# Probabilities times values in one fp32 product: the attention stages of a two-layer encoder trunk without the split of P

## The reference

```
layer 0: u = rms_norm(h)
         z = u @ ab_w_in                  -> q and kv latents, gates, q/k/v of branch B
  "mla": 8 heads, q and k of 96, v of 64, key chunk <= query chunk (64-token chunks)
  "chk": 8 heads, q, k and v of 64, each chunk sees itself and 8 chunks before, plus a bias
         h += [o_a * silu(g_a), o_b * silu(g_b)] @ ab_w_out
layer 1: q, k, v, g, f = rms_norm(h) @ fox_w_in
  "fox": 16 heads of 64, causal, scores + cum[q] - cum[k]
         h += (o_c * silu(g_c)) @ fox_w_out
both:    o = softmax(scores) @ v
         h += (p @ pe_w) * sigmoid(rms_norm(h) @ pe_gate_w)
```

## Time and profile before

| what | value |
|---|---|
| median of three runs | 1998.39 us |
| the profiled execution, and its span | 1996.7 us, 1994.9 us |
| mean granted TensorE clock | 0.956 |
| PE busy | 1783.1 us (89%), 12720 matmuls |
| PE weight loads busy | 1637.5 us (82%) |
| VectorE, ScalarE, GpSimd busy | 955.8 us (48%), 827.3 us (41%), 98.3 us (5%) |
| attention stages, first score to the next stage's first matmul | mla 455 to 625, chk 625 to 800, fox 1460 to 1764 |

### The profile page before, as it was taken

How to read it: one execution, slowest core, us unless ns; L and a number is a source line. 1 busy time by engine, 2 the same in 40 slices (tenths; PEclk the granted TensorE clock), 3 DMA queues, 4 the chain that set the end, 5 groups by cost and what they waited for, 6 DMA issues and landing times. The chain is left out here.

```text
span 1994.9 us, 31875 instructions
## 1 busy us (share of the span) xinstructions
PE 1783.1 (89%) x12720; PEld 1637.5 (82%) x12720; DVE 955.8 (48%) x1797; ACT 827.3 (41%) x1702; POOL 98.3 (5%) x55
## 2 busy tenths in 40 slices
PE   5999778988996996999989999999968988869998
PEld 5999767867884775999988999998757777769898
DVE  5454556105774665234345444331057777722631
ACT  4433234215773675123153332312157878711410
POOL 0000000000210111000000000000002112100000
PEclk9999989998996998999999999999989999989999
DMA  5054468416424551510123433453174555251111
GB/s 179 22 197 143 119 160 220 122 56 171 127 75 111 138 129 42 184 54 27 49 106 106 127 123 119 131 138 102 45 178 122 142 138 129 64 180 48 64 64 38
DMA packets 178372, 223.94 MB, mean 112 GB/s; under 512 B 12857, under 2 KB 148297, under 8 KB 178225
## 3 DMA queue, kind: packets, MB, share of 16 engines
q1 hardware_dynamic: 177152, 218.43, 38.1%
q0 software_dynamic: 640, 2.62, 0.4%
q10 hardware_dynamic: 432, 0.85, 0.1%
HBM read 150.34 MB, written 77.29 MB: 114 GB/s over the span
## 5 line engine op out<-in xcount | busy, mean ns | idle before, releaser
L1562 PE MATMUL m_acc<-m_w_hi,g_a_hi 128*128 128x256 f32 (+1 forms) x1280 | 370.6, 290 | 19.0 <-DVE m_w_lo L179 14.6
L1562 PE MATMUL m_acc<-m_w_hi,g_a_lo 128*128 128x256 f32 (+1 forms) x1280 | 365.5, 286 | 0.0
L1562 PE MATMUL m_acc<-m_w_lo,g_a_hi 128*128 128x256 f32 (+1 forms) x1280 | 364.6, 285 | 0.0
L1562 PEld LDWEIGHTS m_acc<-m_w_hi,g_a_hi 128*128 128x128 f32 x1280 | 246.0, 192 | 19.4 <-DVE m_w_lo L179 14.7
L1562 PEld LDWEIGHTS m_acc<-m_w_lo,g_a_hi 128*128 128x128 f32 x1280 | 246.8, 193 | 0.0
L1562 PEld LDWEIGHTS m_acc<-m_w_hi,g_a_lo 128*128 128x128 f32 x1280 | 244.6, 191 | 0.0
L611 PE MATMUL pa_acc<-pa_w_hi,g_a_hi 128*128 128x256 f32 (+2 forms) x512 | 156.4, 305 | 15.9 <-DVE pa_w_lo L179 15.9
L1562 PE MATMUL t_acc<-t_w_hi,g_a_hi 128*128 128x256 f32 x512 | 146.9, 287 | 15.2 <-DVE t_w_lo L179 15.2
L611 PE MATMUL pa_acc<-pa_w_hi,g_a_lo 128*128 128x256 f32 (+2 forms) x512 | 151.8, 297 | 0.0
L611 PE MATMUL pa_acc<-pa_w_lo,g_a_hi 128*128 128x256 f32 (+2 forms) x512 | 151.5, 296 | 0.0
L1562 PE MATMUL t_acc<-t_w_hi,g_a_lo 128*128 128x256 f32 x512 | 145.6, 284 | 0.0
(11 more groups left out here) (284 smaller groups left out, 4136.4 us busy)
## 6 DMA issues: line engine op xcount, KB each, us to landing
m_w_raw<-in_fox_w_in SPq DMA_DIRECT2D x16, 1024.0 KB, 6.0
pa_w_raw<-in_ab_w_in SPq DMA_DIRECT2D x10, 1024.0 KB, 5.6
f_v<-m_pr SPq DMA_DIRECT2D x32, 256.0 KB, 2.8
fox_q<-f_q SPq DMA_DIRECT2D x32, 256.0 KB
fox_k<-f_k SPq DMA_DIRECT2D x32, 256.0 KB
fox_v<-f_v SPq DMA_DIRECT2D x16, 512.0 KB, 3.3
s_mq<-pa_xr SPq DMA_DIRECT2D x32, 192.0 KB, 3.0
s_mk<-pa_xr SPq DMA_DIRECT2D x32, 192.0 KB, 3.1
```

The lines of the kernel that those rows point to most:

```text
L1562: last = nc.tensor.matmul(dst, a[:, k, t * P:(t + 1) * P], w[:, k0 + k, 0:n], start=(k == 0 and a is m_hi and w is w_hi), stop=(k == kt - ...
```

## The change

The product with v takes the turned probabilities as they are: one copy `pt` in fp32 per piece, no low part. For each pair (tile, key block) there is one matmul of fp32 operands: `pt` (128 x 128) is stationary, the 64 columns of v are moving, and the output has queries on partitions. In each step the product of tile `s-3` stands in front of the transposes of tile `s-2`. Pieces are copied by ScalarE and VectorE in turn, one instruction each. VectorE multiplies each tile's result by the inverse sum and the gate in one instruction (`take`), and each pair of heads is turned once more by 8 transposes (`turn_o`, in two halves) and split into `g_a_hi` and `g_a_lo` (`give`). GpSimd has no work in the attention stages.

In front of the attention, v is stored in one piece of 256 columns per unit (no VectorE instruction, half the bytes), and gates are stored with tokens on partitions: two parts of 256 columns with tokens stationary in place of one of 512. The first head's q and k are loaded in two halves (`in_qk`, then `in_rest`).

```diff
-            v = sp.sb("v", [P, 2, ST, P], F32R)
-            pt_hi = sp.sb("pt_hi", [P, 2, WIDE // P + chk, 2 * P], F32R)
-            pt_lo = sp.sb("pt_lo", [P, 2, WIDE // P + chk, 2 * P], F32R)
+            v = sp.sb("v", [P, 2, ST, P])
+            pt = sp.sb("pt", [P, 3, WIDE // P, P])
...
+                        if hd == 0:
+                            load_qk(0, slice(0, HALF), in_qk[0])
+                        else:
+                            wait(sync, scored, NT * (hd - 1))
+                            load_qk(hd, slice(0, S), in_qk[hd % 2])
...
-                            ins = nc.tensor.matmul(pv[:, uu % 2, 0, cols], v[:, b, j, :], part[:, u % 2, j - lo0, cols],
-                                                   start=(m == 0), stop=(m == len(terms) - 1))
+                        wait(pe, taken, s - 1)
+                        wait(pe, act_copied, act_upto[s])
+                        wait(pe, dve_copied, dve_upto[s])
+                        for j in range(lo, t + 1):
+                            ins = nc.tensor.matmul(pv[:, s % 2, 0:64], pt[:, s % 3, j - lo, :],
+                                                   v[:, m % 2, j, 64 * b:64 * b + 64], start=(j == lo), stop=(j == t))
...
-                        if s >= 5 and s % 2 == 1:
-                            times_v((s - 5) // 2, True)
-                        if 0 <= s - 2 < TILES:
-                            turn_p(s - 2)
-                        if 4 <= s < TILES + 4 and s % 2 == 0:
-                            spread_sums((s - 4) // 2)
-                            times_v((s - 4) // 2, False)
+                        if 0 <= s - 3 < TILES:
+                            times_v(s - 3)
+                        for g in turns_at[s]:
+                            if ring[g][0] == "p":
+                                turn_p(g)
+                            else:
+                                turn_o(g)
...
+                    def copy_p(g):
+                        _, s, js = ring[g]
+                        dve.wait_ge(turned, g + 1)
+                        wait(dve, pv_done, s - 2)
+                        at = js[0] - lowest(s % NT)
+                        nc.vector.tensor_copy(pt[:, s % 3, at:at + len(js), :], turn[:, g % 2, 0:len(js), :])\
+                            .then_inc(dve_copied, 1)
...
+                        nc.vector.scalar_tensor_tensor(out=o[:, m % 2, t, cols], in0=pv[:, s % 2, 0:64],
+                                                       scalar=inverse[:, s % 4:s % 4 + 1], in1=gate[:, m % 2, t, cols],
+                                                       op0=ALU.mult, op1=ALU.mult).then_inc(taken, 1)
```

More of the change, by code:

```diff
@@ L1014, in score @@
                         ins.then_inc(scored, 1)
-                    def turn_p(s):
-                        t = s % NT
-                        lo = lowest(t)
-                        pe.wait_ge(exped, s + 1)
-                        for n, js in enumerate(turned(t)):
-                            g = piece(s) + n
-                            wait(pe, pt_lo_done, g - 1)
-                            for m, j in enumerate(js):
-                                last = nc.tensor.transpose(turn[:, g % 2, m, :], prob[:, s % 3, (j - lo) * P:(j - lo + 1) * P],
-                                                           ident[:])
-                            last.then_inc(pieces_turned, 1)
@@ new lines, in turn_o, with times_v @@
+                    def turn_o(g):
+                        _, m, half = ring[g]
+                        pe.wait_ge(taken, 2 * NT * m + NT + 4 * half + 4)
+                        turn_ready(g)
+                        for n in range(4):
+                            last = nc.tensor.transpose(turn[:, g % 2, n, :], o[:, m % 2, 4 * half + n, :], ident[:])
+                        last.then_inc(turned, 1)
+                    def times_v(s):
+                        hd, t = divmod(s, NT)
+                        m, b, lo = hd // 2, hd % 2, lowest(t)
+                        if t == 0 and b == 0:
+                            pe.wait_ge(in_v[m % 2], 16 * (m // 2 + 1))
+                        wait(pe, taken, s - 1)
[4 more added lines that the diff above has]
+                                                   v[:, m % 2, j, 64 * b:64 * b + 64], start=(j == lo), stop=(j == t))
+                        ins.then_inc(pv_done, 1)
@@ L1071, in exp @@
                         act.wait_ge(maxed, s + 1)
-                        if not chk:
-                            wait(act, pieces_turned, piece(s - 2) if s >= 3 else 0)
-                        src = prob[:, s % 3, 0:n] if chk else scores[:, t % 2, 0:n]
+                        if s >= 3:
+                            act.wait_ge(turned, ring_upto[s - 3])
+                        wait(act, inverted, s - 3)
+                        src = prob[:, s % 3, 0:n] if chk else scores[:, s % 2, 0:n]
                         nc.scalar.activation(prob[:, s % 3, 0:n], src, ACT.Exp, bias=neg_max[:, s % 4:s % 4 + 1],
@@ L1099, in give @@
[L1099 to L1110 removed]
+                                             accum_out=total[:, s % 4:s % 4 + 1]).then_inc(exped, 1)
@@ L1111, in _ @@
+                    for s in steps:
+                        for g in turns_at[s]:
+                            if g in act_of:
+                                copy_p(g)
+                            elif g in o_of:
+                                give(g)
                         if s < TILES:
                             exp(s)
-                        m = s // (2 * NT) - 1
-                        if s % (2 * NT) == 9 and m >= 0:
-                            give(m)
-                    give(NPAIR - 1)
@@ L1198, in stage_attention @@
+                            invert(s - 2)
+                        for g in turns_at[s]:
+                            if g in dve_of:
+                                copy_p(g)
+                            elif g in o_of:
+                                give(g)
+                        if 0 <= s - 3 < TILES:
+                            take(s - 3)
             sp.end()
```

387 lines of the change are left out of this document (149 added, 238 removed).

## The result

| | before | after |
|---|---|---|
| median of the runs, us | 1996.5 (1991.2 to 2003.3) | 2152.0 (2123.5 to 2172.5) |
| after / before | | 1.073, 95% interval 1.062 to 1.084 |
| profiled execution: time, span, us | 1996.7, 1994.9 | 2153.8, 2152.0 |
| TensorE's granted clock over the span | 0.956 | 0.902 |

The kernel became 7.3% slower (the ratio is one of means, without the slowest run of the changed kernel; the medians alone give 7.8%). The forecast was 2048 us, with a range of 1925 to 2290: the sign is right, the size is a third of what happened. The narrower range that went with the forecast's own case, 2020 to 2120, missed.

The account below looks back on a forecast made before the run. TensorE's stream plus gaps bounds the attention stages. Net +84.4, gates +3.1, v -4.5, gaps -12, starts -9 and ends -12 give +50.0 us on 1996.7: 2046.7, median 2048 us, range 1925 to 2290.

Parts of the forecast that it names:

- the forecast's own case: Attention products: each fp32 product needs two loads, 0.224 us; 2048 us, own range 2020 to 2120, chance 0.38.
- So the stages are bound by TensorE's stream, plus gaps in it: mla, chk and fox: PE is the fullest engine, 141.8 of 150, 149.3 of 158 and 253.2 of 285 us busy.
- The price of a product: Product with v in the attention stages: two loads at 0.112, 0.224 us each, 247.3 us for 1104 products.
- Rivals A: Attention products: fp32 product is cheap, one load or two that hide, 0.112 to 0.124 us; 1923 to 1936 us, chance 0.34.
- rival B: Attention products: four loads for each fp32 product, 0.448 us; 2294 us, chance 0.21.
- the one without overlap: Attention products: loads and products of one fp32 instruction do not overlap, 0.33 us each; 2165 us, upper side of the forecast.
- The gap term: Attention stages: the 47.9 us wait before transposes goes, 12 come back as products waiting for copies, 1.1 us a head.
- rival C: Each head's steps: new order makes products wait for copies, +12 and +58 us; 2006 us with the cheap price, chance 0.07.
- Starts, -9: First score of the three attention stages: half the bytes in front saves 3 us each.
- Ends, -12: Tail of the three attention stages: about 6 us instead of 9.98 in fox, so -4 us each.
- Gates and v: Projection stages: gate matmuls split into 256 columns cost +3.1 us; v's dropped subtractions save 4.5 us on PE.
- the net of +84.4: TensorE in attention: 247.3 for products plus 14.3 for output transposes, less 148.5 and 28.7 for what goes, in us.

Follow-up runs that it names:

- e5: Changed kernel with 128 instead of 64 columns of v moving per product in all three attention stages: 2046.9 us.
- e2: Changed kernel with 128 columns of v moving per product in chk alone, same loads: 2049.5 us.
- e7: Changed kernel plus one extra matmul of 512 columns in front of each of chk's 64 sets of products: 2072 and 2075 us in two runs, 2143 in two.
- e3: Changed kernel with pt and v as float32r, so each product is one load and one matmul of 64 columns, low bits dropped: 2054.4 us.
- e6: Changed kernel with pt and v as float32r (one pass) and 128 columns of v moving in all three stages: 2016 to 2021 us in three runs, 1971 in one.
- e1: Changed kernel plus 32 overwritten matmuls of 512 columns in front of each attention stage's first score: 2127 to 2132 us in three runs, 2030 in one.
- e9: Changed kernel, 64 columns of v, with the newer tile's transposes put back in front of the older tile's product: 2128.9 us.
- e8: e5 with the newer tile's transposes put back in front of the older tile's product: 1991.8 us.
- e12: e8 with pt and v as float32r, an extra 512-column matmul before each of chk's product sets, and 32 before each stage's first score: 1892.7 us.
- e10: e8 with the first head's q and k of each stage loaded whole in front of v: 1994.5 us.
- e11: e8 plus 32 extra matmuls of 512 columns in front of each attention stage's first score: 1983.0 us.
- e4: Kernel before the change plus 32 extra matmuls of 512 columns in front of each attention stage's first score: 1982.9 us.

## Why the prediction was wrong, step by step

- **What was missing: TensorE's clock in chk, +105 us.** The prediction took every duration at full clock and had no term, and no rival, for a clock that falls. Its own rows had the hint: chk stood at 0.88 when mla and fox stood at 0.97 and 0.99. The step that failed is "So the stages are bound by TensorE's stream, plus gaps in it", which left the speed of that stream out; so the forecast had chk go "from 158 to about 172", and by the stage table it grew by 110 us, at 0.50. The change made the moving operand of a product 64 columns wide instead of mostly 256. With 128 (e5) the 105 us are gone. That more columns under the same loads bring the clock back in chk is shown by e2 and e5: the mean clock was 0.957 to 0.969 in all their eight runs, against 0.893 to 0.918. e7 did it with columns beside the product, for certain in the one run with a trace. Taking columns away together with loads (e3) made fox fall too, and one pass of 128 (e6) sat at 0.50 in chk as two of 64 did. The gap is not needed for the fall (e1, three runs of four), and the waits are excluded (e9). How many columns are enough, and where, isn't shown: streams with the same instructions left 0.50 at different times.
- **The price of a product was right.** Two loads and two matmuls, 0.225 us against 0.224. Rivals A and B, and the one without overlap, fall on the counts and on the distance between neighbours. e6 confirms it from outside: the second halves are worth at least 28.6 us in mla and 61.1 in fox, 0.099 and 0.106 each. By the Trainium skill (FP8 and Floating Point Precision, section TensorE Precision Notes), true FP32 takes four passes; with a load for each it came to an estimated 0.427 us. The trace has two loads and two matmuls for a product, and half of that time, and the measurement decides: a load for each of four passes is not what this chip did here. Whether the two matmuls hold four passes, no row shows.
- **The gap term had the wrong sign.** Its first half held: the wait in front of the transposes of fox is gone (31.1 us before, 0.0 after), in the new order and in the old one (e8). "so 12 us of the 47.9 come back" failed in its second half: the order with the product in front costs 55 us against the other (e5, e8), not 36, so the gaps are +7 and not -12. It is rival C's mechanism, smaller than C drew it (36 + 58 us). The forecast had put 1.1 us on a head; over 32 heads it is 1.7, in fox 2.4: there are some four waits of half a microsecond a head there (62 in fox, 31.3 us by the loads), not one at its start. And the new order had nothing to cover: with it undone hardly a wait comes back (0.0 us in front of fox's transposes in e8, and 1.7 in e12, whose product is half as long). The order was never weighed against the old one in the new kernel.
- **Starts, -9: at most -2.7** (e10), and not told apart from nothing. The first load's issue to the first score of fox was forecast at 7 us and came at 6.0, so fox's own start gained 4; most of the gain does not arrive in the total, and why isn't shown.
- **Ends, -12: right.** From the last transpose of probabilities to the end of the last subtraction it was 9.98 us in fox before and is 5.6 now, forecast about 6. In mla it went from 9.98 to 5.6 too, in chk from 9.2 to 6.3 (at 0.50): -11.7 in all.
- **Gates and v:** with their share of the starts, the stages that hold them were to lose 1.5 (up to mla) and 6.0 us (m); they lost 4.6 and 8.9. The second is right to 3 us. The first shows little: the same code up to mla took 450.0 to 455.2 us in the traces of the changed kernel, e5 and e8, and 454.9 before.
- **A sum that fits by luck.** e5, close to full clock, takes 2046.9 us, and the forecast's sum was 2046.7. But the gaps are 19 us worse than it says and the starts at least 6, so other terms must be some 25 us too dear. e11 and e4 show the same: there neither the new waits nor the clock differ, the terms that remain give 84.4 + 3.1 - 4.5 - 47.9 - 9 - 12 = +14.1 (with the starts at -2.7, +20.4), and +0.2 was measured. Where these 20 us sit, none of the runs shows; the net of +84.4 is the largest term and may hold them, though its price of a product is right.

The range held the time, because rival B reached to it, for a reason that has nothing to do with B: that was luck.

## What to carry to other kernels

Read the granted clock of each stage beside its busy share before anything is summed: a PE that is 99% busy can run at half speed. Where an operand is made so narrow that loads pace the stream, try moving more columns under the same loads: here it cost nothing that showed (e5) and brought the clock back. And weigh a reordering inside the new kernel, not the old one: the durations that made a wait appear may be gone.

## What was not expected of the hardware

- A stream with hardly a gap, PE busy 258.56 of 260 us, stayed at 0.50 from its first to its last matmul; another 64 columns in each half product, under the same loads, brought it to 1.00 within 20 us and 102 us off the kernel.
- A clock of 1.00 that was carried over the gap fell in such a stream by itself after about 25 us (e1), while in the kernel before it was held to chk's end (e4).
- The same kernel can have two times, and its mean clock goes with them: e7 2072 us at 0.953 and 2143 at 0.917, e6 1971 at 0.937 and 2016 at 0.910, e1 2030 at 0.975 and 2130 at 0.920.
